# SyncE issues the rotary step's partition-swapping DMAs; the norms' broadcasts and the modulation's columns become TensorE transposes, with sums on VectorE

## The chip, the cores and the metric

The kernel runs on one NeuronCore of a Trainium2 chip. Its time is device microseconds of one launch; the median of three runs stands for a kernel.
## The reference, cut to what matters

One decoder block over a sequence of 1024 tokens with 1024 features, all in float32:

```
mod = silu(c) @ w_ada + b_ada            # 9 sections of 1024, and 2 more for the end
h = rmsnorm(x, g1) * (1 + sc1) + sh1
x = x + 0.5 * gt1 * (silu(h @ w1) * (h @ w3)) @ w2          # feed-forward 1
h = rmsnorm(x, g2) * (1 + sc2) + sh2
q, k, v, B, C, u = split(h @ w_in)
q, k = rope(q), rope(k)                  # t * cos + rotate_half(t) * sin, 64-wide heads
o = (softmax(q1 k1') - lam * softmax(q2 k2')) v             # 4 heads, causal, 128-query blocks
y = B * conv3(C * u)                     # 8 channel groups
x = x + gt2 * concat(rmsnorm(o), rmsnorm(y)) @ w_out
h = rmsnorm(x, g3) * (1 + sc3) + sh3
x = x + 0.5 * gt3 * (silu(h @ w1b) * (h @ w3b)) @ w2b       # feed-forward 2
out = rmsnorm(x, gf) * (1 + scf) + shf
```

## The kernel before, in words

Features lie on the 128 partitions and tokens along the free dimension, in two halves of 512. Large products are split in float32r parts (a rounded high part and the rest), three matmuls of 512 columns for one product; ScalarE makes the high parts and VectorE the low ones. Each engine's order is written out by hand, and semaphores with constant counts tie the engines together. The stages are: a start (about 43 us) with the first norm and the first modulation sections; feed-forward 1 (`up(0)`, then `down(0)`); the convolution groups with their projections; projections of the first head's q and k and of v; four attention heads, `body(hh, ...)`, in whose steps i = 0 to 7 TensorE also projects the next head's q and k; the output projection; feed-forward 2 and the last norm. Matmuls of the feed-forwards stand on line 1536, all others on line 1532, attention's transposes on lines 1956 and 1882.

**The modulation.** During `up`, one section at a time, VectorE multiplies eight loaded tiles of w_ada by the entries of silu(c) and adds them up in `AdaSum` (128 partitions x 1024; 72 tiles, nine sections: six in feed-forward 1, three in 2). What is left is a sum over partitions. `ada_cols` does it on TensorE between two jobs of `up`: eight matmuls of a 128x128 block of `AdaSum` with a column of ones give eight columns in bank 7 of PSUM. Two steps later `ada_bias` on VectorE adds the bias from there (line 1294). A float32 matmul is two MATMUL rows in the profile; a transpose is one.

**The norms.** `mean(q)` sums squares over partitions, ScalarE takes the root, VectorE the reciprocal, and `Spread` holds it repeated over 128 columns. `bcast(q)` (eight uses) and `group_bcast(q)` (eight, in the convolution stage) multiply four 128x128 blocks of `Spread` by the identity `ident`, a part of the tile `Square`, so that every partition gets the row of factors; VectorE then multiplies by it (`nm`, `norm_mul`, and line 1430 for the groups).

**The rotary step.** For head m, part j (two halves each of q and k): ScalarE copies the projection from PSUM into `TmpA` (`raw`, line 871). Then four DMAs swap neighbouring groups of 32 partitions into `TmpG` or `TmpA[:, 1]` (`exchange`, line 877), issued by ScalarE from its own instruction list. GpSimd multiplies with cosines and sines and adds (lines 569, 571, 574). In `body` the four parts fall into the steps i = 1, 2, 4, 5. ScalarE's other work there: exponentials (`exps`, line 899, TensorE's next scores wait for them), copies of transposed blocks (951), of outputs (905), squares (911) and the splitting of a weight unit (`split_hi`, 760). SyncE's list in this stage held only the loads of 29 weight units `Mr` (line 483), each waiting for an older unit to be split.

Of the kernel before, what the change touches and what calls it, by code (L numbers as in the profile page):

```python
# [150 lines left out]
def program(nc, up_w, down_w, units, ada, x_t, cols_d, lam_d, rope_d, square_d, out_t):  # L151
    ctx = ExitStack()
    with ctx:
# [85 lines left out]
        Cols, _ = place("Cols", [P, NCOLS])  # L239
        Mod, _ = place("Mod", [P, SECTIONS * KT])  # L240
        Scale, _ = place("Scale", [P, 4, KT])
        Gate, _ = place("Gate", [P, 3, KT])
# [117 lines left out]
        ada_used, row_used, row_done = sem("ada_used"), sem("row_used"), sem("row_done")  # L360
        cols_done, mod_done, scales = sem("cols_done"), sem("mod_done"), sem("scales")
        lam_done, lam_exp = sem("lam_done"), sem("lam_exp")
# [37 lines left out]
        def _(sp):  # L400
# [79 lines left out]
            sp.dma_start(Rope[:], rope_d).then_inc(rope_loaded, 16)  # L480
            for n in range(RING, UNITS):
                sp.wait_ge(lo_done, n - RING + 1)
                sp.dma_start(Mr[:, n % RING, :], units[n]).then_inc(raw_loaded[n % RING], 16)
            for u in range(2):
                load_up(1, u)
# [114 lines left out]
        def _(act):  # L600
# [272 lines left out]

            def exchange(j, slot, to):

                for a in range(0, P, 32):
                    act.dma_start(to[a:a + 32, :], TmpA[a ^ 32:(a ^ 32) + 32, slot, :]).then_inc(shifted[j % 2], 16)  # L877

            for c in (1, 2):  # L880
                split_hi(U_Q0 + c, job_done, JOBS["v"])
            for j in range(4):
                raw(0, j, 4 + j, JOBS["v"] + j + 1, j % 2, 2)
                act.wait_ge(rraw, j + 1)
                if j >= 2:
                    act.wait_ge(rope_done, j - 1)
                exchange(j, j % 2, TmpG[:, j % 2, :])
                if j % 2:
                    split_hi(U_Q0 + 3 + j // 2, job_done, JOBS["v"] + j + 1)
# [33 lines left out]
            def body(hh, prev, nxt):  # L923

                J, nq, steps = JOBS["att"] + 4 * hh, U_Q1 + 2 * hh, STEP_OF_JOB
                for i in range(QB):
# [26 lines left out]
                    if nxt and i == QB - 1:  # L953
                        exps(0, at + 1)
                    rotated = nxt and i in steps
                    if rotated:
                        act.wait_ge(rraw, hh * 4 + 4 + j + 1)
                        act.wait_ge(rope_done, hh * 4 + 4 + j)
                    if i:
                        square_o(i - 1, at - 1)  # L960
                    if rotated:
                        exchange(j, 0, TmpA[:, 1, :])
                    if rotated and j % 2:
                        split_hi(nq + 2 + j // 2, job_done, J + j + 1)
# [29 lines left out]
        def _(dve):  # L994
# [295 lines left out]

            def ada_bias(s, bank=7):

                dve.wait_ge(cols_done, s + 2 if s else 2)
                nc.vector.tensor_tensor(Mod[:, bass.ts(s, KT)], PS[:, bank, 0:KT], Cols[:, bass.ts(s, KT)], ALU.add)\
                    .then_inc(mod_done, 1)
# [86 lines left out]
            second_bias(0)  # L1382
            ada_bias(SH1, 4)
            second_scale(0)
# [145 lines left out]
        def _(pe):  # L1530
# [7 lines left out]
            def ada_between(ph, t):  # L1538

                for y in range(KT - 1, KT * len(ADA_IN[ph]), KT):  # L1540
                    if ada_step(ph, y) + 2 == t:
                        if y == KT - 1:
                            pe.wait_ge(silu_done, silu_no(ph, 0, 3))
                        ada_cols(ADA_IN[ph][y // KT])
# [79 lines left out]
            def down_free(ph, i, d):  # L1624

                if i >= 2:
                    pe.wait_ge(x_added, 28 * ph + 4 * (i - 2) + d + 1)
                elif i == 0:
                    if d == 0:
                        pe.wait_ge(silu_done, silu_no(ph, NG - 1, 2))  # L1630
                    elif d == 1:
                        pe.wait_ge(dadd, dadd_no(ph, PAIRS - 2, 5))
                    elif d == 2:
                        pe.wait_ge(dadd, dadd_no(ph, PAIRS - 1, 5))
                    else:
                        pe.wait_ge(mul_done, silu_no(ph, NG - 1, 2))
                elif d == 0:
                    pe.wait_ge(mul_done, silu_no(ph, NG - 2, 2))
                elif d == 1:
                    pe.wait_ge(dadd, dadd_no(ph, PAIRS - 3, 5))  # L1640
                elif d == 3:
                    pe.wait_ge(mod_done, 12 if ph else 9)
# [95 lines left out]
            def bcast(q):  # L1738

                pe.wait_ge(spread_done, q + 1)  # L1740
                for b in range(4):
                    made = mm(PS[:, 7 - q % 2, blk(b)], Spread[:, q % NH, blk(b)], ident, True, True)
                made.then_inc(bcast_done, 1)

            def ada_cols(s, bank=7):

                pe.wait_ge(ada_used, (s + 1) * KT)
                for c in range(KT):
                    made = mm(PS[:, bank, c:c + 1], AdaSum[:, blk(c)], Ones[:], True, True)
                made.then_inc(cols_done, 1)  # L1750
# [32 lines left out]
            for cg in range(2):  # L1783
# [287 lines left out]
```

## Time and profile before

| | |
|---|---|
| median of 3 runs | 1884.25 us (1883.03 to 1886.19) |
| the profiled execution's own time | 1886.2 us |
| its span in the trace | 1884.4 us |
| busy: PE, PEld | 1815.4 us (96%), 1470.0 us |
| busy: DVE, ACT, POOL | 1260.8, 773.4, 270.8 us |
| mean granted clock of TensorE | 0.986 |

The span is the time from the first to the last instruction; the rest of an execution's time lies around it. An engine's busy time is not counted while it issues DMAs or waits.

### The profile page before, as it was taken

What the parts mean: (1) busy time and instruction counts of PE and PEld (TensorE: products, weight loads), DVE (VectorE), ACT (ScalarE), POOL (GpSimd) and SP (SyncE); (2) the same over time, 40 slices, a digit from 0 to 9 for tenths busy, and PEclk for the clock granted to TensorE, in tenths of its full rate; (3) what the DMA queues carried; (4) which work ended last, traced back from release to release, by engine and by line L of the source; (5) the groups of instructions that cost most, each with busy time, mean ns of one, the idle gap of its engine ahead of it and who ended that gap; (6) DMA issues with size and microseconds to landing.
All of it is one profiled execution on the core that took longest, in us unless ns stands there. A gap on an engine that the chain in (4) does not pass through costs nothing.

```text
span 1884.4 us, 22925 instructions
## 1 busy us (share of the span) xinstructions
PE 1815.4 (96%) x8248; PEld 1470.0 (78%) x8248; DVE 1260.8 (67%) x1952; ACT 773.4 (41%) x1392; POOL 270.8 (14%) x411
## 2 busy tenths in 40 slices
PE   5999999999999999999999999899999999999997
PEld 2878888888788877888877666787888888888885
DVE  5887777777586776444226668687767766577767
ACT  5643333333344564111125555574333333344445
POOL 2011211211210000000303330201111211111000
PEclk9999999999999999999999999999999999999998
DMA  8165565654864321111201110325454544476432
GB/s 319 69 229 199 206 224 188 242 202 171 272 217 150 96 75 61 44 45 45 77 26 44 45 34 1 134 82 209 157 195 170 207 166 172 167 255 218 128 96 90
DMA packets 100528, 269.76 MB, mean 143 GB/s; under 512 B 13120, under 2 KB 13504, under 8 KB 100288
## 3 DMA queue, kind: packets, MB, share of 16 engines
q1 hardware_dynamic: 62608, 146.30, 22.3%
q0 software_dynamic: 34304, 117.46, 17.9%
q10 hardware_dynamic: 3504, 4.53, 1.0%
q8 instruction: 66, 1.08, 0.2%
q14 instruction: 46, 0.38, 0.1%
HBM read 209.53 MB, written 54.53 MB: 140 GB/s over the span
## 4 chain that ended last, share of the span: by engine, by line
PE 87%; DVE 6%; ACT 3%; issue 1%; DMA 1%; POOL 1%; ACTq 1%; DVEq 0%; POOLq 0%
PE PS L1536 60%; PE PS L1532 26%; DMA AdaFirst<-ada 1%; PE PS L1956 1%; DVE NMax L1447 1%; ACTq L877 1%; DVE Ml L1246 1%; DVE SqSum L1312 0%; DVE TmpA L1330 0%; DVE Wl L1041 0%; DVE Wl L1038 0%; DMA TmpA<-TmpA 0%; DVE CT L1412 0%; ACT PR L899 0%; DVE X L1193 0%
## 5 line engine op out<-in xcount | busy, mean ns | idle before, releaser
L1536 PE MATMUL PS<-Bh,Wh 128*128 128x512 f32 x1120 | 438.0, 391 | 3.8 <-ACT T L659 3.8
L1536 PE MATMUL PS<-Bh,Wl 128*128 128x512 f32 x1120 | 436.6, 390 | 0.0
L1536 PE MATMUL PS<-Bl,Wh 128*128 128x512 f32 x1120 | 436.5, 390 | 0.0
L1536 PEld LDWEIGHTS PS<-Bh,Wh 128*128 128x128 f32 x1120 | 210.5, 188 | 50.1 <-issue 4.1
L1536 PEld LDWEIGHTS PS<-Bh,Wl 128*128 128x128 f32 x1120 | 210.6, 188 | 44.4
L1536 PEld LDWEIGHTS PS<-Bl,Wh 128*128 128x128 f32 x1120 | 210.6, 188 | 43.2
L1536 PE MATMUL PS<-Wh 128*128 128x512 f32 x616 | 240.3, 390 | 3.4 <-DVE Wl L1041 1.7
L1536 PE MATMUL PS<-Wl,Wh 128*128 128x512 f32 x616 | 239.7, 389 | 0.0
L1536 PE MATMUL PS<-Wh,Wl 128*128 128x512 f32 x616 | 239.7, 389 | 0.0
L1038 DVE TENSOR_TENSOR Wl<-RawB,Wh 128x512 fp32r<-128x512 f32 x154 | 106.6, 692 | 135.9 <-ACT Wh L634 134.8
L634 ACT ACTIVATE Wh<-RawB 128x512 fp32r<-128x512 f32 x154 | 97.3, 632 | 229.8 <-PE PS L1536 229.8
L659 ACT ACTIVATE T<-PS 128x512 f32<-128x512 f32 x120 | 71.7, 597 | 248.4 <-PE PS L1536 248.4
L1006 DVE TENSOR_TENSOR Wl<-Sums,Wh 128x512 fp32r<-128x512 f32 x160 | 110.2, 689 | 83.1 <-ACT Wh L624 82.9
L1536 PEld LDWEIGHTS PS<-Wh 128*128 128x128 f32 x616 | 115.6, 188 | 28.4 <-DVE T L1072 2.5
L1536 PEld LDWEIGHTS PS<-Wl,Wh 128*128 128x128 f32 x616 | 115.6, 188 | 24.0
L1536 PEld LDWEIGHTS PS<-Wh,Wl 128*128 128x128 f32 x616 | 115.6, 188 | 24.0
L1532 PE MATMUL PS<-Hh,Mh 128*128 128x512 f32 x320 | 131.9, 412 | 2.2 <-DVE Hl L1336 1.3
L1006 DVE TENSOR_TENSOR Wl<-Raw,Wh 128x512 fp32r<-128x512 f32 x136 | 93.9, 695 | 57.3 <-ACT Wh L624 57.1
L624 ACT ACTIVATE Wh<-Sums 128x512 fp32r<-128x512 f32 x160 | 98.4, 623 | 79.3 <-DVE Sums L1024 65.0
L1532 PE MATMUL PS<-Hl,Mh 128*128 128x512 f32 x320 | 126.9, 397 | 0.0
L1532 PE MATMUL PS<-Hh,Ml 128*128 128x512 f32 x320 | 126.9, 397 | 0.0
L1062 DVE TENSOR_TENSOR T<-T,PS 128x512 f32<-128x512 f32 x120 | 82.1, 684 | 42.0 <-PE PS L1536 38.8
(193 smaller groups left out, 2866.8 us busy)
## 6 DMA issues: line engine op xcount, KB each, us to landing
Raw<-up_w SPq DMA_DIRECT2D x86, 512.0 KB, 5.5
Ada<-ada POOLq DMA_DIRECT2D x72, 512.0 KB, 4.5
g_dram<-T SPq DMA_DIRECT2D x88, 256.0 KB, 2.1
W2s<-down_w POOLq DMA_DIRECT2D x88, 256.0 KB, 4.3
s_dram<-W2s POOLq DMA_DIRECT2D x88, 256.0 KB, 2.5
GQ<-g_dram POOLq DMA_DIRECT2D x88, 256.0 KB, 3.3
RawB<-s_dram SPq DMA_DIRECT2D x88, 256.0 KB, 2.8
RawB<-down_w SPq DMA_DIRECT2D x66, 256.0 KB, 2.7
```

The lines of the kernel that those rows point to most:

```text
L624: nc.scalar.activation(Wh[:, slot, :], src, ACT.Copy).then_inc(w_hi, 1)
L634: nc.scalar.activation(Wh[:, 4 + m % 4, :], RawB[:, m % 8, :], ACT.Copy).then_inc(w_hi, 1)
L659: nc.scalar.activation(T[:, 4 * w + q, :], PS[:, x + (j == 1), :], ACT.Copy).then_inc(acopy, 1)
L877: act.dma_start(to[a:a + 32, :], TmpA[a ^ 32:(a ^ 32) + 32, slot, :]).then_inc(shifted[j % 2], 16)
L1006: nc.vector.tensor_tensor(Wl[:, slot, :], src, Wh[:, slot, :].bitcast(F32), ALU.subtract).then_inc(w_lo, 1)
L1038: nc.vector.tensor_tensor(Wl[:, 4 + m % 4, :], RawB[:, m % 8, :], Wh[:, 4 + m % 4, :].bitcast(F32), ALU.subtract).then_inc(w_lo, 1)
L1062: nc.vector.tensor_tensor(T[:, 4 * w + q, :], T[:, 4 * w + q, :], PS[:, x + (j != 4), :], ALU.add)\
L1246: nc.vector.tensor_tensor(lo, Mr[:, n % RING, :], hi.bitcast(F32), ALU.subtract).then_inc(lo_done, 1)
L1447: nc.vector.tensor_reduce(NMax[:, c:c + 1], scores(c, 0, i + 1), AX.X, ALU.max, negate=True)\
L1532: return nc.tensor.matmul(out, lhs, rhs, start=first, stop=last)
L1536: return nc.tensor.matmul(out, lhs, rhs, start=first, stop=last, skip_group_check=True)
L1956: made = nc.tensor.transpose(PS[:, 4 + r, blk(b % 4)], PR[:, 2, blk(b)], ident)
```

## The change

TensorE's `bcast` and `group_bcast` call `transpose` with the same operands in place of a matmul with the identity. `ada_cols` transposes the eight blocks of `AdaSum` (128x128 each) into banks 6 and 7 of PSUM; VectorE sums them along the free dimension into `ModSum` and then adds the bias, as two instructions with a semaphore between them. The first section (`AdaRow`, bank 4) and `second_cols` stay as they were. The `exchange` DMAs go from ScalarE's list to SyncE's, between the loads of weight units; their waits go with them.

```
@@ SyncE
-            for n in range(RING, UNITS):
+            def load_unit(n):
                 sp.wait_ge(lo_done, n - RING + 1)
                 sp.dma_start(Mr[:, n % RING, :], units[n]).then_inc(raw_loaded[n % RING], 16)
+            def exchange(m, j):
+                slot, to = (0, TmpA[:, 1, :]) if m else (j % 2, TmpG[:, j % 2, :])
+                sp.wait_ge(rraw, 4 * m + j + 1)
+                if m:
+                    sp.wait_ge(rope_done, 4 * m + j)
+                elif j >= 2:
+                    sp.wait_ge(rope_done, j - 1)
+                for a in range(0, P, 32):
+                    sp.dma_start(to[a:a + 32, :], TmpA[a ^ 32:(a ^ 32) + 32, slot, :]).then_inc(shifted[j % 2], 16)
+            for n in range(RING, U_Q0 + 6):
+                load_unit(n)
+            for m in range(HEADS):
+                for j in range(4):
+                    exchange(m, j)
+                    n = (U_Q1 + 3 + 2 * m if m else U_Q0 + 6) + j // 2
+                    if j % 2 and n < UNITS:
+                        load_unit(n)
+                if m == 0:
+                    for n in range(U_Q0 + 8, U_Q1 + 5):
+                        load_unit(n)
@@ ScalarE, head 0 and body
-                act.wait_ge(rraw, j + 1)
-                if j >= 2:
-                    act.wait_ge(rope_done, j - 1)
-                exchange(j, j % 2, TmpG[:, j % 2, :])
...
-                    rotated = nxt and i in steps
-                    if rotated:
-                        act.wait_ge(rraw, hh * 4 + 4 + j + 1)
-                        act.wait_ge(rope_done, hh * 4 + 4 + j)
                     if i:
                         square_o(i - 1, at - 1)
-                    if rotated:
-                        exchange(j, 0, TmpA[:, 1, :])
-                    if rotated and j % 2:
+                    if nxt and i in steps and j % 2:
                         split_hi(nq + 2 + j // 2, job_done, J + j + 1)
@@ VectorE
+            def ada_bias(s):
+                dve.wait_ge(cols_done, s + 2)
+                nc.vector.tensor_reduce(ModSum[:], PS[:, 6:8, :].rearrange("p b (c d) -> p (b c) d", d=P), AX.X, ALU.add)\
+                    .then_inc(mod_sum, 1)
+                dve.wait_ge(mod_sum, s - 1)
+                nc.vector.tensor_tensor(Mod[:, bass.ts(s, KT)], ModSum[:], Cols[:, bass.ts(s, KT)], ALU.add)\
                     .then_inc(mod_done, 1)
@@ TensorE
-                    made = mm(PS[:, 7 - q % 2, blk(b)], Spread[:, q % NH, blk(b)], ident, True, True)
+                    made = nc.tensor.transpose(PS[:, 7 - q % 2, blk(b)], Spread[:, q % NH, blk(b)], ident)
...
-                    made = mm(PS[:, bank, c:c + 1], AdaSum[:, blk(c)], Ones[:], True, True)
+                    made = nc.tensor.transpose(PS[:, 6 + c // 4, blk(c % 4)], AdaSum[:, blk(c)], ident)
...
-                        made = mm(PS[:, 7, blk(b)], Spread[:, q % 2, blk(b)], ident, True, True)
+                        made = nc.tensor.transpose(PS[:, 7, blk(b)], Spread[:, q % 2, blk(b)], ident)
...
-                            pe.wait_ge(silu_done, silu_no(ph, 0, 3))
+                            pe.wait_ge(mul_done, silu_no(ph, 0, 3))
...
-                elif d == 3:
+                elif d == 2:
                     pe.wait_ge(mod_done, 12 if ph else 9)
```

ScalarE's list in head 0, steps i = 2 and 3, before the change (`PR` exponentials, `O` output copy, `DT` transposed block, `Mh` high part of a weight unit; a row is one call, x4 four equal ones):

```order
L871 ACTIVATE TmpA_108<-PS 128x512
L905 ACTIVATE O_89<-PS,RSum_128 128x128
L951 ACTIVATE DT_110<-PS 128x384
L911 ACTIVATE Junk_130,SqO_131<-O_89 128x128
L877 DMA TmpA_108<-TmpA_108 32x512 x4
L760 ACTIVATE Mh_85<-Mr_90 128x1024
L899 ACTIVATE PR_104,Sum_127<-PS,NMax_126 128x640 x2
```

The same place after it:

```order
L896 ACTIVATE TmpA_108<-PS 128x512
L920 ACTIVATE O_89<-PS,RSum_129 128x128
L966 ACTIVATE DT_110<-PS 128x384
L926 ACTIVATE Junk_131,SqO_132<-O_89 128x128
L785 ACTIVATE Mh_85<-Mr_90 128x1024
L914 ACTIVATE PR_104,Sum_128<-PS,NMax_127 128x640 x2
```

The four DMAs, and the two waits ahead of them, no longer stand between the copy of the projection and the unit's split and the next exponentials. They stand in SyncE's list, here from the last load ahead of them to the second head's (before: one row, 29 loads in a row):

```order
L485 DMA Mr<-units 128x1024 x19
L496 DMA TmpG<-TmpA 32x512 x8
L485 DMA Mr<-units 128x1024
L496 DMA TmpG<-TmpA 32x512 x8
L485 DMA Mr<-units 128x1024 x4
L496 DMA TmpA<-TmpA 32x512 x8
L485 DMA Mr<-units 128x1024
```

Each pair of parts (eight DMAs) now lies between two unit loads, and waits for them and they for it. VectorE's list around the bias of the seventh modulation section in `up(1)` (`T` sums of feed-forward products, `Sums` and `Wl` weights in preparation), before:

```order
L1006 TENSOR_TENSOR Wl<-Sums,Wh 128x512
L1062 TENSOR_TENSOR T<-T,PS 128x512
L1294 TENSOR_TENSOR Mod<-PS,Cols 128x8
L1024 TENSOR_TENSOR Sums<-Raw 128x512
L1006 TENSOR_TENSOR Wl<-Sums,Wh 128x512
L1062 TENSOR_TENSOR T<-T,PS 128x512
```

And after:

```order
L1015 TENSOR_TENSOR Wl<-Sums,Wh 128x512
L1071 TENSOR_TENSOR T<-T,PS 128x512
L1308 TENSOR_REDUCE ModSum<-PS 128x8
L1311 TENSOR_TENSOR Mod<-ModSum,Cols 128x8
L1033 TENSOR_TENSOR Sums<-Raw 128x512
L1015 TENSOR_TENSOR Wl<-Sums,Wh 128x512
L1071 TENSOR_TENSOR T<-T,PS 128x512
```

One reduction over 128x1024 is new between two sums that TensorE's next jobs wait for; nothing changed places.

## Rows read from the trace of the kernel before

**Rows 1.** The page's chain that ended last: share of the span by engine.

```profile
PE 87%; DVE 6%; ACT 3%; issue 1%; DMA 1%; POOL 1%; ACTq 1%; DVEq 0%; POOLq 0%
```

**Rows 2.** Windows: length, busy PE, PEld, DVE, ACT, POOL (instructions), clock, DMA share, GB/s.

```profile
100.00:480.00 380.00, 379.81 (x1716) 315.04 (x1715) 279.91 (x403) 134.50 (x236) 75.36 (x140) 1.00 0.59 209
982.00:1037.00 55.00, 52.26 (x276) 38.89 (x273) 35.25 (x67) 28.49 (x76) 17.43 (x13) 0.97 0.14 39
1037.00:1092.00 55.00, 50.32 (x262) 36.82 (x261) 34.79 (x64) 30.09 (x79) 17.35 (x13) 0.97 0.14 39
1092.00:1147.00 55.00, 48.08 (x260) 35.03 (x258) 37.87 (x69) 32.31 (x82) 16.88 (x12) 1.00 0.11 30
1277.00:1650.00 373.00, 372.98 (x1669) 309.11 (x1668) 252.51 (x377) 132.42 (x234) 62.54 (x116) 1.00 0.50 178
```

**Rows 3.** Groups of instructions on PE: count, busy us, mean ns, idle before.

```profile
L1532 PE MATMUL PS<-Ones,AdaSum 128*128 128x1 f32 x160 | 18.6, 245 | 0.0
L1532 PE MATMUL PS<-Square,Spread 128*128 128x128 f32 x128 | 18.1, 287 | 1.0 <-DVE Spread L1321 1.0
```

**Rows 4.** Timeline of PE at a section's columns: start, us, instruction.

```profile
163.19 1.84 PE L1532 MATMUL PS<-Ones,AdaSum 128*128 128x1 f32 x16
164.89 0.49 PE L1536 MATMUL PS<-Bh,Wh 128*128 128x512 f32 x1
```

**Rows 5.** Timeline of PE at eight float32 transposes in attention.

```profile
1034.23 1.06 PE L1882 MATMUL PS<-Square,O 128*128 128x128 f32 x8 [0.16 <-DVE O L1468]
1035.05 0.48 PE L1532 MATMUL PS<-Hh,Mh 128*128 128x512 f32 x1
```

**Rows 6.** Timeline of PE at a group's broadcast.

```profile
741.98 1.05 PE L1532 MATMUL PS<-Square,Spread 128*128 128x128 f32 x8
742.79 0.48 PE L1532 MATMUL PS<-Hh,Mh 128*128 128x512 f32 x1
```

**Rows 7.** Chain in order of time: start and convolution stages.

```profile
17.91 18.84 PE PS L1532 x56
...
735.48 7.57 PE PS L1532 x40
...
750.42 27.30 PE PS L1532 x128
```

**Rows 8.** Timeline, the last norm's broadcast.

```profile
1872.86 2.08 PE L1532 MATMUL PS<-Square,Spread 128*128 128x128 f32 x8 [1.03 <-DVE Spread L1321]
```

**Rows 9.** Timeline of ACT in head 0, steps i = 2 and 3.

```profile
994.79 0.51 ACTq L877 DMA_DIRECT2D TmpA<-TmpA  x1
995.33 2.25 ACTq L877 DMA_DIRECT2D TmpA<-TmpA  x3
997.69 1.06 ACT L760 ACTIVATE Mh<-Mr 128x1024 fp32r<-128x1024 f32 x1 [2.54 <-issue]
```

**Rows 10.** Timeline of PE, the scores behind it in three heads.

```profile
999.57 0.69 PE L1532 MATMUL PS<-QK 64*128 64x512 f32 x1 [0.90 <-ACT PR L899]
...
1053.04 1.47 PE L1532 MATMUL PS<-NextK,NextQ 64*128 64x512 f32 x3 [1.11 <-ACT PR L899]
...
1107.66 0.69 PE L1532 MATMUL PS<-QK 64*128 64x512 f32 x1 [0.85 <-ACT PR L899]
```

**Rows 11.** Groups of instructions on DVE: widest reduction from PSUM, and bias.

```profile
L1447 DVE TENSOR_REDUCE NMax<-PS 128x1 f32<-128x1024 f32 x8 | 9.8, 1224 | 0.3
L1294 DVE TENSOR_TENSOR Mod<-PS,Cols 128x8 f32<-128x8 f32 x10 | 1.6, 160 | 4.5 <-PE PS L1532 4.5
```

**Rows 12.** Timeline of DVE and PE at two biases in `up`.

```profile
480.08 0.69 DVE L1038 TENSOR_TENSOR Wl<-RawB,Wh 128x512 fp32r<-128x512 f32 x1 [8.82 <-ACT Wh L634]
...
1395.77 0.16 DVE L1294 TENSOR_TENSOR Mod<-PS,Cols 128x8 f32<-128x8 f32 x1
...
1397.89 0.69 DVE L1062 TENSOR_TENSOR T<-T,PS 128x512 f32<-128x512 f32 x1
...
1400.41 0.39 PE L1536 MATMUL PS<-Bh,Wh 128*128 128x512 f32 x1
```

More of the change, by code:

```diff
@@ L240, in program @@
         Mod, _ = place("Mod", [P, SECTIONS * KT])
+        ModSum, _ = place("ModSum", [P, KT])
         Scale, _ = place("Scale", [P, 4, KT])
@@ L360, in program @@
         ada_used, row_used, row_done = sem("ada_used"), sem("row_used"), sem("row_done")
-        cols_done, mod_done, scales = sem("cols_done"), sem("mod_done"), sem("scales")
+        cols_done, mod_sum, mod_done, scales = sem("cols_done"), sem("mod_sum"), sem("mod_done"), sem("scales")
         lam_done, lam_exp = sem("lam_done"), sem("lam_exp")
@@ L872, in raw @@
                                      scale=DH ** -0.5 if j < 2 else 1.0).then_inc(rraw, 1)
-            def exchange(j, slot, to):
-                for a in range(0, P, 32):
-                    act.dma_start(to[a:a + 32, :], TmpA[a ^ 32:(a ^ 32) + 32, slot, :]).then_inc(shifted[j % 2], 16)
             for c in (1, 2):
@@ L1289, in second_scale, with first_bias @@
                                                col("g1", KH * n, KH), ALU.add, ALU.mult).then_inc(scales, 1)
-            def ada_bias(s, bank=7):
-                dve.wait_ge(cols_done, s + 2 if s else 2)
-                nc.vector.tensor_tensor(Mod[:, bass.ts(s, KT)], PS[:, bank, 0:KT], Cols[:, bass.ts(s, KT)], ALU.add)\
+            def first_bias():
+                dve.wait_ge(cols_done, 2)
+                nc.vector.tensor_tensor(Mod[:, 0:KT], PS[:, 4, 0:KT], Cols[:, 0:KT], ALU.add).then_inc(mod_done, 1)
+            def ada_bias(s):
[4 more added lines that the diff above has]
+                nc.vector.tensor_tensor(Mod[:, bass.ts(s, KT)], ModSum[:], Cols[:, bass.ts(s, KT)], ALU.add)\
                     .then_inc(mod_done, 1)
@@ L1382, in _ @@
             second_bias(0)
-            ada_bias(SH1, 4)
+            first_bias()
             second_scale(0)
@@ L1741, in bcast, with ada_cols @@
                 for b in range(4):
-                    made = mm(PS[:, 7 - q % 2, blk(b)], Spread[:, q % NH, blk(b)], ident, True, True)
+                    made = nc.tensor.transpose(PS[:, 7 - q % 2, blk(b)], Spread[:, q % NH, blk(b)], ident)
                 made.then_inc(bcast_done, 1)
-            def ada_cols(s, bank=7):
+            def ada_cols(s):
                 pe.wait_ge(ada_used, (s + 1) * KT)
                 for c in range(KT):
-                    made = mm(PS[:, bank, c:c + 1], AdaSum[:, blk(c)], Ones[:], True, True)
+                    made = nc.tensor.transpose(PS[:, 6 + c // 4, blk(c % 4)], AdaSum[:, blk(c)], ident)
                 made.then_inc(cols_done, 1)
```

## The prediction

> **What bounds the kernel now.** I read the page's chain first: 87% of the span is TensorE, 6% VectorE, 3% ScalarE [rows 1]. So an instruction that leaves TensorE's list is worth its whole length wherever TensorE does not wait anyway, and an instruction that leaves another engine is worth nothing unless TensorE stood waiting for it. Then I asked for the stretches. In the two `up` stages TensorE is busy 379.81 of 380 us and 372.98 of 373 us, VectorE about 280 and 253 us [rows 2]. There all nine modulation sections are summed. In the three attention stretches that also carry projections, TensorE is idle 2.7, 4.7 and 6.9 us of 55 [rows 2]: what ScalarE, VectorE and GpSimd do can show there, and only there up to that much. Last I went to the places that the edit touches.
>
> **Columns of the modulation: matmuls become transposes.** From the first column matmul of a section to the feed-forward matmul behind it, 1.70 us pass (163.19 to 164.89) for 16 MATMUL rows [rows 4]. They have one column each, so it is their 128x128 weight loads that take the time. Afterwards there are 8 rows, of 128 columns. This kernel has the same thing in attention: eight float32 transposes take 0.82 us from their start to that of the next matmul (1034.23 to 1035.05) [rows 5]. So a section saves 1.70 - 0.82 = 0.88 us. Nine sections: 7.9 us, all in stretches in which TensorE has no idle time to absorb it. Of the 160 rows of this kind [rows 3], 144 go; the other 16 belong to the second section's `second_cols` and stay.
>
> **What it adds on VectorE.** A reduction over 128x1024 from PSUM takes 1.22 us where the kernel has one already, and the bias stays at 0.16 us [rows 11]; with the wait between the two I count 1.3 us more a section, 11.7 us in all. I cost it at nothing, because something covers it: VectorE has 100 us free in the first `up` and 120 us in the second [rows 2]. The cover must hold locally too. TensorE's tight wait is for the sum `T` of two jobs before. The bias nearest ahead of such a sum is that of the seventh section: bias at 1395.77, sum 1397.89 to 1398.58, and the job that waits for it starts at 1400.41 [rows 12], 1.83 us later. With 1.3 us more ahead of it, less what VectorE idled, the sum is still in time. The other tight place is at the end of `up(0)`, where the kernel's last bias comes before VectorE's 8.82 us of idling [rows 12]. If the cover were gone, each section would cost up to 1.3 us on TensorE; zero is the one end, 11.7 us the other, and I take zero.
>
> **Broadcasts: half the rows.** A broadcast has 8 MATMUL rows, 0.81 us from its start to the next matmul (741.98 to 742.79) [rows 6]; 128 rows are 16 broadcasts [rows 3]. Afterwards there are 4. By the transposes (0.82 us for eight, 0.10 to 0.11 us each) [rows 5], 0.38 to 0.4 us stay, so 0.42 us is saved at full clock. Which of the 16 lie on the path? The two at the start stand inside an unbroken TensorE piece, 17.91 + 18.84 us [rows 7]; I take 0.6 us for both and not 0.84, since what follows starts at the low clock and may cover more of it. In the convolution stage the chain runs through TensorE up to each group's multiplication by the broadcast (pieces of 7.57 and 27.30 us are two of them) [rows 7], so all eight count; so do that of the second half's norm ahead of this stage and the two around the output projection: 11 x 0.42 = 4.6 us. The last one runs at 1.2 GHz with nothing behind it but the end: 2.08 us for eight rows [rows 8], of which a fixed 0.24 us is the pipeline's (1.05 against 0.81 in [rows 6]); half the rest is 0.9 us. The two in the last part of each `down` lie beside a long chain of ScalarE and VectorE work: between 0 and 0.84 us, I take 0.4. Sum: 0.6 + 4.6 + 0.9 + 0.4 = 6.5 us.
>
> **Partition swaps leave ScalarE.** In head 0, step i = 2, ScalarE issues from 994.79 to 997.58, then splits a weight unit from 997.69, and only then makes the exponentials [rows 9]; TensorE's scores at 999.57 wait 0.90 us for them, and in the next two heads 1.11 and 0.85 us at the same place [rows 10]. Without the DMAs (2.8 us) the exponentials are early, and those gaps close: 2.9 us. Lower bound nothing, if VectorE's maxima, which ScalarE also needs, come as late; upper bound the gaps themselves, as TensorE is the bound on both sides of them. The other idle time of the stretches [rows 2] belongs to VectorE's chain at step i = 6 and to the head change, where no swap stands ahead: unchanged. The issue time itself, some 2.5 us for each of 16 swaps, is worth no more than this, for ScalarE is busy only about half of those stretches [rows 2]. On SyncE the swaps wait between unit loads. Queued behind a late load would be the swap, GpSimd's rotation and the next head's first scores; behind a late swap a load. Every load there waits for the split of a unit that is done before the next part's projection, and the swap may now start at the copy's end, not behind ScalarE's other work. I take zero for it.
>
> **The sum** against the profiled execution's own 1886.2 us: 7.9 + 6.5 + 2.9 = 17.3 us, so 1868.9 us. That execution was 1.95 us above the median of the runs shown; I apply the sum to the median: 1884.25 - 17.3 = 1867 us, 0.9% faster.
>
> **Rivals.**
> *The swaps give nothing* (another wait, the maxima or GpSimd, fills the same gaps): 1867 + 2.9 = 1870 us. For it: VectorE is as busy as ScalarE there [rows 2]. Against it: the 2.54 us before the split is issuing alone [rows 9].
> *VectorE becomes late* in `up`, and TensorE waits in every section: 1.3 us x 9 = 11.7 us lost, 1879 us. For it: tight waits exist at all; against it: 1.83 us of room and 26% free [rows 2, 12].
> *The clock, which ends on the other side.* TensorE's granted clock is 1.0 through both `up` stages and 0.97 in two attention stretches [rows 2]: 3% of 55 us is 1.65 us lost in a stretch with one fall. Attention's stretches hold the kernel's only transposes, idle gaps too. If a run of transposes let the clock fall each time as there, at 25 places instead of none, it would cost 25 x 1.65 = 41 us: 1867 + 41 = 1908 us. It decides from 13 such falls on ((17.3 + 3.8) / 1.65). Against it: three stretches with 36 and more transposes each have two falls among them, and the third, with as many transposes and the most idle time, has clock 1.00 [rows 2].
> The Trainium skill ("TensorE: Matmul & The Clock Gate", Part 4, PE-mode transpose) says that transposes do not count as TensorE work for its clock, which would speak for this rival. By that rule alone the time is the rival's; by the rows, in which full-rate transposes stand in a stretch at 1.00, it is the sum's.
> *The transposes don't save* (a float32 transpose as long as the two rows it replaces): only the swaps remain, 1884.25 - 2.9 = 1881 us. Against it stands the direct row, 0.82 us for eight [rows 5].
>
> **How the numbers follow.** The sum as it stands 0.68; swaps give nothing 0.15; VectorE late in part or whole 0.08; clock falls at many places 0.06, half of these slower than before; transposes don't save 0.03. The measurement of this kernel tells a change from none at about 0.2%, 3.8 us. Faster by more than that: the first three and a part of the rest, 0.93; within it 0.03; slower 0.04. Falls of the clock come and go with the gaps around them: one or two, 1.65 us each, either way, which with the two open terms of 0.4 us spans 1863 to 1871 for the likeliest case alone. With the swaps giving nothing and a fall too (1873.5), and VectorE's term in part, the range is 1862 to 1875 us.
>
> **What would show it.** In the profile after: eight MATMUL rows with `AdaSum` a section, about 0.8 us to the next feed-forward matmul, no new TensorE idle behind them and a clock of 1.00 in `up`; a reduction of about 1.22 us with `ModSum` on VectorE; four rows with `Spread` a broadcast in 0.4 us; no DMA rows on ScalarE in attention, and no wait of the scores for exponentials at step i = 3 in three heads. I am wrong if new idle time appears before feed-forward jobs with VectorE's `T` as its releaser, if the granted clock falls in `up`, or if GpSimd's rotation waits longer for SyncE's swaps than for ScalarE's and the next head's first scores wait for it.

## The result, and the profile after

| | before | after |
|---|---|---|
| median, runs side by side | 1884.03 us (1883.03 to 1886.19, 4 runs) | 1860.4 us (1858.88 to 1863.07, 4 runs) |
| ratio, 95% interval | | 0.9872, 0.9857 to 0.9887 |
| the profiled execution | 1886.19 us | 1858.88 us |
| its span, mean granted clock | 1884.4 us, 0.986 | 1857.1 us, 0.991 |
| busy: PE, DVE, ACT, POOL | 1815.4, 1260.8, 773.4, 270.8 us | 1788.9, 1271.0, 774.3, 268.2 us |

The change gains 23.6 us, 1.3%. The forecast was 1867.0 us, with a range from 1862 to 1875 us: the direction holds, and the time lies below the range. The two profiled executions stand 27.3 us apart, more than the medians; how far single executions of one kernel differ is shown under experiments 12 to 16.

The windows of the profile after (columns as in [rows 2]: length, busy us of PE, PEld, DVE, ACT, POOL, then the granted clock), for the first `up`, three attention stretches and the second `up`:

```profile
100.00:480.00 380.00, 379.76 (x1697) 314.03 (x1697) 292.01 (x419) 135.96 (x239) 75.95 (x141) 1.00 0.60 210
969.00:1020.00 51.00, 48.08 (x265) 35.28 (x262) 32.89 (x64) 28.04 (x75) 16.16 (x12) 1.00 0.15 42
1020.00:1071.00 51.00, 47.76 (x262) 34.97 (x261) 35.60 (x65) 30.25 (x77) 16.52 (x12) 1.00 0.15 42
1071.00:1122.00 51.00, 48.29 (x263) 35.44 (x262) 34.69 (x67) 30.40 (x77) 16.17 (x12) 1.00 0.12 32
1255.00:1627.00 372.00, 371.98 (x1652) 307.50 (x1651) 257.06 (x381) 132.88 (x234) 62.78 (x117) 1.00 0.50 178
```

TensorE is still busy all through both `up` stages, at clock 1.00: VectorE's new reductions bring it no wait, and no fall of the clock stands at the nine runs of transposes. Groups of instructions after, answering to [rows 3, 11] (count, busy us, mean ns, idle before):

```profile
L1766 PE MATMUL PS<-Square,AdaSum 128*128 128x128 f32 x72 | 9.3, 272 | 0.0
L1308 DVE TENSOR_REDUCE ModSum<-PS 128x8 f32<-128x1024 f32 x9 | 11.0, 1219 | 1.8 <-PE PS L1766 1.8
L1311 DVE TENSOR_TENSOR Mod<-ModSum,Cols 128x8 f32<-128x8 f32 x9 | 1.5, 168 | 0.3
L1819 PE MATMUL PS<-Square,Spread 128*128 128x128 f32 x32 | 4.8, 272 | 0.0
L1759 PE MATMUL PS<-Square,Spread 128*128 128x128 f32 x32 | 5.5, 298 | 1.5 <-DVE Spread L1338 1.5
```

PE's timeline after (start, length, instruction) at the places of [rows 4, 6, 8], a section, a group's broadcast and the last norm:

```profile
161.73 1.03 PE L1766 MATMUL PS<-Square,AdaSum 128*128 128x128 f32 x8
162.52 0.48 PE L1553 MATMUL PS<-Bh,Wh 128*128 128x512 f32 x1
...
734.23 0.60 PE L1819 MATMUL PS<-Square,Spread 128*128 128x128 f32 x4
734.58 0.48 PE L1549 MATMUL PS<-Hh,Mh 128*128 128x512 f32 x1
...
1846.53 1.11 PE L1759 MATMUL PS<-Square,Spread 128*128 128x128 f32 x4 [1.03 <-DVE Spread L1338]
```

From its first transpose to the matmul behind it a section takes 0.79 us (162.52 - 161.73) in place of 1.70, a broadcast 0.35 in place of 0.81, the last one 1.11 in place of 2.08.

ScalarE's timeline after, in head 0 at the steps of [rows 9]:

```profile
980.46 0.19 ACT L926 ACTIVATION_READ_ACCUMULATOR Junk<-O 128x1 f32 x1
980.55 1.05 ACT L785 ACTIVATE Mh<-Mr 128x1024 fp32r<-128x1024 f32 x1
982.34 0.80 ACT L914 ACTIVATE PR<-PS,NMax 128x640 f32<-128x640 f32 x1 [0.74 <-DVE NMax L1464]
```

The split follows at once, and ScalarE now waits 0.74 us for VectorE's maxima, so these come next in line, as one rival had it, but early enough. PE's scores behind it in three heads, answering to [rows 10]:

```profile
985.80 1.57 PE L1549 MATMUL PS<-QK 64*128 64x512 f32 x8
987.30 0.50 PE L1549 MATMUL PS<-Hh,Mh 128*128 128x512 f32 x1
...
1036.97 1.57 PE L1549 MATMUL PS<-NextK,NextQ 64*128 64x512 f32 x8
...
1088.04 1.57 PE L1549 MATMUL PS<-QK 64*128 64x512 f32 x8
```

No wait is left. And the rows say more than that: all eight score matmuls are through in 1.57 us.

**Where the time went.** The clock of TensorE blurs such a comparison, as the experiments show. I therefore compare with a second profile of the kernel before (e_before_2 below, span 1880.3 us), whose granted clock was 0.5 for 17.1 us in all between 60 and 1830 us, near the 13.7 us of the profile after. Each stretch runs between the same two matmuls in both (start to start); both have clock 1.00 all through it:

| stretch | before | after | saved | forecast |
|---|---|---|---|---|
| six sections in the first `up` | 105.31 to 479.16 | 103.70 to 471.96 | 5.6 us | 5.3 |
| three sections in the second | 1253.60 to 1806.18 | 1233.75 to 1783.66 | 2.7 us | 2.6 |
| six of the eight groups' broadcasts | 775.71 to 902.94 | 765.50 to 890.16 | 2.6 us | 2.5 |
| from head 0's step i = 2 to head 2's end | 996.79 to 1131.24 | 985.60 to 1113.02 | 7.0 us | 2.9 |

The spans differ by 23.2 us. Of the 5.3 us outside these stretches 1.4 us are net effects of falls of the clock that only one of the two has (+1.5, -1.6 and +1.5 us at three places); what is left, 3.9 us, I put down to the other ten broadcasts (forecast 4.0); it is a remainder, in which differences at the start and at the clock's falls are mixed. So columns gave 8.3 us (forecast 7.9), broadcasts 6.5 (6.5), of which 2.6 are read directly, and the partition swaps 7.0 (2.9).

### The profile page after: what moved, and what is told of

Read it like the earlier page. It is cut to its first block, busy times and chain, and to the rows that moved or that the text cites. A ratio compares the mean times of both kernels' runs of the same rounds, so it can differ in the third digit from the quotient of the medians.

```text
span 1857.1 us, 22662 instructions
## 1 busy us (share of the span) xinstructions
PE 1788.9 (96%) x8112; PEld 1445.0 (78%) x8112; DVE 1271.0 (68%) x1961; ACT 774.3 (42%) x1392; POOL 268.2 (14%) x411
## 3 DMA queue, kind: packets, MB, share of 16 engines
q8 instruction: 65, 1.06, 0.2%
## 4 chain that ended last, share of the span: by engine, by line
PE 86%; DVE 8%; ACT 3%; issue 1%; DMA 1%; POOL 0%; ACTq 0%; DVEq 0%; POOLq 0%
PE PS L1553 60%; PE PS L1549 24%; DVE NMax L1464 1%; PE PS L1973 1%; DMA AdaFirst<-ada 1%; DVE X L1360 1%; DVE SqSum L1329 1%; DVE Ml L1255 1%; DVE TmpA L1347 1%; DVE Wl L1050 0%; PE PS L1766 0%; DVE Wl L1047 0%; DVE Wl L1015 0%; DVE X L1202 0%; DVE PR L1478 0%
## 5 line engine op out<-in xcount | busy, mean ns | idle before, releaser
L571 POOL DMA_DIRECT2D s_dram<-W2s x88 | 48.2, 547 | 412.8 <-DVE W2s L1093 412.8
```

The costliest lines, as they stand in the source:

```text
L571: pool.dma_start(s_dram[ph][x // 4, n], W2s[:, n, :]).then_inc(w2_stored[n], 16)
```

## Experiments

Each kernel was timed in turn with the kernel before on the same chip. "The parts" are the change's own pieces.

**1 to 3. One part at a time on the kernel before.** e_cols has only the changes of `ada_cols` and `ada_bias` and their semaphores, e_bcast only `transpose` in `bcast` and `group_bcast`, e_swap only the diff's SyncE and ScalarE parts.

> The kernel before with the modulation's columns alone changed (transposes into banks 6 and 7, reduction and bias on VectorE). Theory A, the gain is the shorter TensorE insertion and nothing else: 0.91 us in each of nine sections, 8.2 us, so about 1876 us; granted clock 1.00 in both up stages, no new idle time behind the sections. Theory B, part of the surplus over my sum comes from the clock (fewer falls once the transposes are in): more than 8.2 us, by steps of 1.65 us. Theory C, VectorE's extra 11.7 us costs something: less than 8 us.

> The kernel before with the 16 broadcasts alone changed. Theory A: 0.45 us for each broadcast on the path: two at the start, eight groups, three norms, and about 0.9 us for the last, 6.5 to 7 us, about 1877.5 us. Theory B, the broadcasts change where the clock falls (convolution stage, end): up to 1.65 us more or less for each fall gained or lost.

> The kernel before with the partition swaps alone moved to SyncE. Theory A (my prediction's): the three gaps of TensorE at step i = 3 close, 2.9 us, about 1881 us. Theory B: the second map's scores were late there too; with both exponentials in time the two maps' score matmuls start together (as in the changed kernel, 985.80 and 985.81 us), 0.76 us a head more, so 5.4 us, about 1878.6 us. Either way a fall of the clock in attention may go as well, 1.65 us each.

| | median | ratio, 95% interval | saved |
|---|---|---|---|
| e_cols | 1876.37 us (7 runs) | 0.9949, 0.9930 to 0.9968 | 7.9 us |
| e_bcast | 1876.48 us (5 runs) | 0.9959, 0.9946 to 0.9971 | 7.8 us |
| e_swap | 1876.08 us (5 runs) | 0.9958, 0.9946 to 0.9970 | 8.2 us |

The medians add up to 23.9 us, near the change's gain of 23.6; each has an uncertainty of some 2 to 4 us (the seven runs of e_cols alone spread from 1868.69 to 1879.78 us). Columns agree with their forecast; the broadcasts' 6.5 us lies inside their interval (5.5 to 10.2 us); the swaps' 2.9 us lies outside theirs (5.7 to 10.2 us). So the miss is mainly in the swaps, and they show it without the other parts. The traces say the same, stretch by stretch of the table above, against e_before_2: in e_cols the two stretches with the nine sections are 8.3 us shorter, in e_bcast the six groups 2.6 us and in e_swap the three heads 7.9 us (126.53 us in place of 134.45), while in all three kernels the sections and groups that the part doesn't touch take the same time within 0.1 us. Only the three heads of e_cols and e_bcast, each with one fall of the clock in them, take 1.0 and 0.8 us less without a reason that I looked for.

**Why the swaps give more: the trace.** PE's timeline at the scores of the three heads in e_before_2, to be held against the changed kernel's above:

```profile
998.08 2.33 PE L1532 MATMUL PS<-QK 64*128 64x512 f32 x8 [1.01 <-ACT PR L899]
1000.34 0.50 PE L1532 MATMUL PS<-Hh,Mh 128*128 128x512 f32 x1
...
1051.48 2.33 PE L1532 MATMUL PS<-NextK,NextQ 64*128 64x512 f32 x8 [1.20 <-ACT PR L899]
...
1104.74 2.33 PE L1532 MATMUL PS<-QK 64*128 64x512 f32 x8 [0.98 <-ACT PR L899]
```

The same eight matmuls take 2.26 us to the next one before (998.08 to 1000.34), and 1.50 us after (985.80 to 987.30). They are the scores of two softmax maps, four each, with 64 rows of the array apiece, and each map's matmuls wait for that map's exponentials. After, both maps' matmuls start together (985.80 and 985.81), before, the second 0.53 us behind the first (998.08 and 998.61), since it waits for the second exponentials. Views of PE that end 0.2 to 0.3 us behind the block's start show it, e_before_2 and then the changed kernel, where two matmuls have begun:

```profile
998.08 0.69 PE L1532 MATMUL PS<-QK 64*128 64x512 f32 x1 [1.01 <-ACT PR L899]
```

```profile
985.80 0.71 PE L1549 MATMUL PS<-QK 64*128 64x512 f32 x2
```

So late exponentials cost a gap and then a block in which the maps run less side by side: the block ends 1.85, 2.03 and 1.82 us later in the three heads, 5.7 us, of which 0.76 us each, 2.3 us, lie inside the block. The gap itself is not the same in every execution: in head 0 it is 0.90, 1.61, 1.01 and 1.50 us in the four profiles of the kernel before, and the three together are 2.9 to 3.7 us; the block is 2.26 us in the heads of all four.

The remaining 1.3 us of the 7.0 stand at step i = 6. VectorE's timeline there, e_before_2, head 0:

```profile
1019.03 1.95 DVE L1246 TENSOR_TENSOR Ml<-Mr,Mh 128x1024 fp32r<-128x1024 f32 x1
1020.90 0.15 DVE L1454 RECIPROCAL RSum<-Sum 128x2 f32<-128x2 f32 x1
1021.09 0.22 DVE L1456 SCALAR_TENSOR_TENSOR Ratio<-RSum,LamS,Sum 128x1 f32<-128x1 f32 x1
1021.34 1.28 DVE L1461 SCALAR_TENSOR_TENSOR PR<-PR,Ratio 128x1024 f32<-128x1024 f32 x1
```

and GpSimd and PE of the same profile:

```profile
1018.63 1.27 POOL L574 TENSOR_TENSOR NextK<-NextK,TmpA 128x512 f32<-128x512 f32 x1
...
1022.68 1.09 PE L1956 MATMUL PS<-Square,PR 128*128 128x128 f32 x8 [1.26 <-DVE PR L1461]
```

The same places in e_swap:

```profile
1017.19 1.26 POOL L597 TENSOR_TENSOR NextK<-NextK,TmpA 128x512 f32<-128x512 f32 x1
...
1018.50 1.22 DVE L1253 TENSOR_TENSOR Ml<-Mr,Mh 128x1024 fp32r<-128x1024 f32 x1
...
1021.42 1.09 PE L1963 MATMUL PS<-Square,PR 128*128 128x128 f32 x8 [0.53 <-DVE PR L1468]
```

VectorE's split of a weight unit takes 1.22 us when GpSimd has ended before it begins, and 1.95 us when GpSimd's last rotation instruction still runs for 0.87 us (to 1019.90); TensorE waits behind it, 0.53 against 1.26 us. Swaps issued early end the rotation early. The Trainium skill ("SBUF — State Buffer", Who interferes with whom) says that a VectorE instruction with two SBUF inputs contends with a GpSimd instruction that reads SBUF, and calls the ports that they share an exclusive lock. These rows agree: 0.87 us of overlap cost VectorE 0.73 us, and 0.67 us of it in the changed kernel's head 0 cost 0.53 us, while GpSimd's instruction took 1.26 or 1.27 us in each case. In the changed kernel the splits take 1.75, 1.66 and 1.22 us in the three heads and TensorE waits 1.06, 0.98 and 0.53 us, in each case 0.68 or 0.69 us less than the split is long. In e_swap all three take 1.22 us, which is why the swaps gave 7.9 us there and 7.0 us here.

**4. Does VectorE have the room?**

```
+                for n in range(3):
                     nc.vector.tensor_reduce(ModSum[:], ...).then_inc(mod_sum, 1)
...
```

> The changed kernel with VectorE's reduction of each modulation section done three times in a row instead of once, 2.5 us more in each of nine sections. If VectorE's room covers it: no change against the changed kernel, about 1860 us. If the room is only just enough for one reduction: up to 2.5 us x 9 = 22 us more, and TensorE idle before feed-forward jobs with VectorE's sums as releaser.

Measured: 1863.41 us (4 runs), ratio 0.9889 (0.9876 to 0.9902), with 33.0 us of reductions in place of 11.0, and 1.4 to 3.0 us above the changed kernel's two medians. Against the changed kernel's trace TensorE lost time at two of the nine sections, 1.20 and 1.13 us. So I was wrong that three cost nothing, but they cost only a tenth of their 22 us more; that one costs nothing is seen in the stretches above, where each section saved its full 0.9 us.

**5 and 6. Which swap matters?** e_swap_j1 puts only part j = 1 of heads 1 to 3 on SyncE, e_swap_rest all the others and not those three.

```
+        def on_sync(m, j):
+            return m > 0 and j == 1          # e_swap_rest: m == 0 or j != 1
```

> The kernel before with only the part j = 1 of heads 1 to 3 (step i = 2, three of the 16 swaps) issued by SyncE, the other 13 by ScalarE as before. If what the change gains in attention is the lateness of the exponentials of step i = 3 in these three places (gap, second map's scores, and the clock's falls behind them): nearly the whole of what all 16 gave, 5 to 8 us, about 1877 to 1879 us, and no fall of the clock between the attention heads. If ScalarE's issue time is worth something everywhere: about 3/16 of it, 1.5 us.

> The complement: the other 13 swaps issued by SyncE, those three by ScalarE. If the three places are all: about the time of the kernel before, 1884 us, within 1.5 us, TensorE's gaps before the scores of step i = 4 as before. If issue time counts everywhere: 6 us less. A third possibility: the first part's swap, now earlier on SyncE, lets GpSimd end earlier, so that ScalarE waits less for it at step i = 2; then the gaps shrink and some of the gain comes here too.

Measured: 1878.41 us (8 runs), ratio 0.9962 (0.9950 to 0.9975), and 1876.56 us (6 runs), 0.9955 (0.9937 to 0.9973). In both traces the gap before the scores is closed in all three heads. That one part would carry it was wrong as an "only"; the third possibility is what came. Nor did the closed gaps keep the clock up: e_swap_j1's profile has two falls between the attention heads. ScalarE in e_swap_rest shows why the other swaps help as well:

```profile
992.73 0.49 ACT L980 ACTIVATE DT<-PS 128x384 f32<-128x384 f32 x1
992.99 0.60 ACTq L905 DMA_DIRECT2D TmpA<-TmpA  x1
...
995.62 1.06 ACT L788 ACTIVATE Mh<-Mr 128x1024 fp32r<-128x1024 f32 x1 [2.10 <-issue]
996.58 0.78 ACT L928 ACTIVATE PR<-PS,NMax 128x640 f32<-128x640 f32 x1
```

The issuing is still there, but it begins at once. In e_before_2 ScalarE first stood idle for 1.57 us until GpSimd had done with the part ahead:

```profile
993.13 0.31 ACT L911 ACTIVATE Junk<-O 128x128 f32<-128x128 f32 x1 [1.57 <-POOL NextQ L574]
```

In e_swap_rest, with that part's swap on SyncE GpSimd is through by 991.33. The delay had two pieces, a wait of 1.57 us and 2.5 to 2.9 us of issuing, and taking away either closes the gap. The split at i = 6 keeps its 1.95 to 1.98 us in e_swap_j1 and takes 1.22 us in e_swap_rest: that share belongs to the later parts.

**7 and 8. Is it ScalarE's time?** The changed kernel, with n small copies on ScalarE where part j = 1 was issued.

```
+                    if nxt and i in steps and j == 1:
+                        for n in range(8):            # e_work12: 12 here and in the wait
+                            nc.scalar.activation(Extra[:], Rope[:, 0, 0:P], ACT.Copy).then_inc(extra, 1)
+                            act.wait_ge(extra, 8 * hh + n + 1)
```

> The changed kernel with eight small copies (128x128, each waited for, about 2.6 us in all, the length of the four issues) on ScalarE where the swap of part j = 1 stood; they write a tile that nothing reads. If ScalarE's time alone held up the exponentials: the gaps of the kernel before come back, 5.4 us more than the changed kernel and a fall or two of the clock, 1866 to 1868 us. If the wait for GpSimd ahead of the issue was a needed part of it (the changed kernel's exponentials are some 2.2 us early): the first scores are in time and only the second map's late, 0 to 2.3 us more, 1860 to 1863 us.

> The changed kernel with twelve small copies (about 4.0 us, by eight that took 2.69) on ScalarE in each of the three heads where it used to issue a swap and to wait for GpSimd. Removed wait and issues were together 1.57 + 2.8 = 4.4 us; eight copies (2.7 us) brought no gap back. If the gaps come of ScalarE's time before its exponentials and nothing else, there was room of about 3.4 us before PE waits (4.4 less the gap of 0.97): twelve copies bring back 0.4 to 0.8 us a head before the scores and some of the 0.76 us by which the score block was shorter, 1.5 to 4 us in all, so 1862 to 1867 us, and the exponentials of head 0 begin about 1.3 us later than with eight. Rival (the gaps come of the queue or of the DMAs' landing): no gap at all, 1860 to 1864, as with eight.

Measured: 1863.61 us (5 runs), ratio 0.9884 (0.9868 to 0.9900), with no wait before the scores; and 1867.33 us (6 runs), 0.9903 (0.9884 to 0.9921). PE's scores of head 0 with eight copies and with twelve:

```profile
988.81 1.70 PE L1555 MATMUL PS<-QK 64*128 64x512 f32 x8
```

```profile
989.07 2.33 PE L1555 MATMUL PS<-QK 64*128 64x512 f32 x8 [0.66 <-ACT PR L916]
```

Copies of 2.69 us bring no gap and delay the second map by 0.14 us; copies of 4.06 us bring back 0.66 us of gap and the long block, with no DMA on that queue. Relative to the changed kernel this is 0.75 + 0.77 us in head 0's trace. The 5.3 us over the changed kernel timed beside it (e_after_again) are above the upper end of what I expected; 4.5 us of them are the three blocks with their gaps. So ScalarE's time before its exponentials is enough to make the gap and the long block; neither the queue nor the DMAs' landing is needed for it.

**9 and 10. The changed kernel again, and without the swaps.**

> The changed kernel once more, nothing edited. Theory 1 (the mechanism gives about 18 us by the steps between the matmuls of the two traces, and what is over that is stretches at the granted clock of 0.5 that this kernel's executions happen to have fewer of): the median comes within 1860 to 1865 us again, and in the new profiled execution the PE rows before the scores of heads 0 to 2 at query block 4 are without a wait again (score block 1.50 us, not 2.26), while its stretches at 0.5 clock may stand in other places and sum to anything between 14 and 31 us. Theory 2 (the change itself does away with the stretches at 0.5): the new profile again shows only three such stretches, about 14 us, in the same places.

> The changed kernel with ScalarE issuing the partition swaps of the rotary step again; the transposed columns and broadcasts stay. If the parts add up (columns and broadcasts gave 7.9 and 7.8 us by medians when each was alone): 1884.0 - 15.7 = 1868.3 us, so 1866 to 1870.5, and 5 to 8 us above the changed kernel. In the trace the three gaps of 0.9 to 1.1 us before the scores of heads 0 to 2 are back, and the block of eight score matmuls takes 2.26 us again, 5.4 us in all. Rival (the swaps' gain of 8 us seen alone was mostly a matter of the clock): 1863 to 1866, with those gaps back all the same. Rival (the other two parts need the swaps on SyncE, and lose part of their gain without): above 1871.

Measured: e_after_again 1862.04 us (6 runs), ratio 0.9881 (0.9859 to 0.9903); e_no_swap 1873.02 us (6 runs), 0.9929 (0.9907 to 0.9951), 11.0 us more. From the transposes ahead of head 0's scores (982.17, and 979.35 in the changed kernel) to VectorE's `PR` at step i = 6 of head 2 (1120.41 and 1109.81), e_no_swap takes 7.8 us more than the changed kernel, with gaps of 1.96, 1.01 and 0.96 us and the 2.26 us blocks back; head 0's gap is the longest of all profiles. I had forecast 5.4 us, from shorter gaps and without the split of step i = 6, and 1868.3 us; 1873 lies in my rival's zone (parts that need each other), but its interval (1866 to 1874 us) holds both. By these stretches the parts add up; by the times alone it isn't settled.

**11. One block later for VectorE's split.** An attempt at a faster version.

```
-                    if nxt and i - 1 in steps and steps.index(i - 1) % 2:
-                        split_lo(nq + 2 + steps.index(i - 1) // 2)
+                    if nxt and i in (3, QB - 1):
+                        split_lo(nq + 2 + i // (QB - 1))
```

> The changed kernel with VectorE's second split of a head's keys moved one query block later, from before to after the scores whose probabilities wait for VectorE. In the changed kernel's trace PE idles 1.06, 0.98 and 0.53 us in heads 0 to 2 for VectorE's PR, which stands behind that split. Theory: these three close, up to 2.6 us, so 1858 us (1856.5 to 1860.5), if the split is still in time for the next head's scores. Rival (PE waits as long for the next thing, VectorE's DT before it at the head's last step, or the split itself is late for the next head): same as the changed kernel or up to 2 us slower, 1860 to 1863, with the wait moved to the last query block or to the head's change.

Measured: 1863.42 us (6 runs), ratio 0.9878 (0.9855 to 0.9901): as the changed kernel. In the first trace no head has a gap for `PR`, but that is not the edit's doing: its clock fell to 0.5 just ahead of that place in all three heads, and the unedited kernel with the same three falls (e_after_2) has no such gap either. Only head 2 of e_late_split_2 has clock 1.00 there. PE in it, and in the unedited kernel's e_after_again:

```profile
1112.54 1.09 PE L1973 MATMUL PS<-Square,PR 128*128 128x128 f32 x8
1114.99 0.50 PE L1549 MATMUL PS<-Gh,Mh 128*128 128x512 f32 x1 [1.35 <-DVE Ml L1255]
```

```profile
1110.85 1.09 PE L1973 MATMUL PS<-Square,PR 128*128 128x128 f32 x8 [0.53 <-DVE PR L1478]
```

There the edit took away the gap of 0.53 us, and the next matmul waited 1.35 us for the late split, in both traces. So the rival was right for head 2: the wait moved, and grew. What the edit does at clock 1.00 in heads 0 and 1 no trace shows.

**12 to 16. The clock.** The first profiles suggested that the change also rid the kernel of falls of the clock. I looked at more executions of unedited kernels, and once more at e_late_split.

> The kernel before once more, unchanged, for a second profile. If the falls of TensorE's clock in the attention heads follow from the gaps, there are one or two falls between 980 and 1110 us again, though perhaps in other places; if they are chance, there may be none.

> The kernel before, unedited, one more profiled execution, for the stretches at the granted clock of 0.5 between 60 and 1830 us: its two profiles so far have 30.7 and 37.5 us of them. Theory 1 (what the change gained beyond the steps between the matmuls is that its executions have fewer such stretches): 27 us or more again. Theory 2 (chance of which execution was profiled): anything from 14 to 37 us, as with the changed kernel.

> The kernel before, unedited, a further profiled execution: as for the other one, 27 us or more at the granted clock of 0.5 between 60 and 1830 us if the change did away with some of them, anything from 14 to 37 us if the two first profiles differed from the changed kernel's by chance. The span less half of it is 1867 to 1869 us in either case.

> The changed kernel, unedited, one more profiled execution, for its stretches at the granted clock of 0.5 between 60 and 1830 us: its two profiles so far have 13.7 and 20.5 us. Theory 1 (it has fewer of them than before): under 24 us again. Theory 2 (chance): anything from 14 to 37 us. Under both, the span less half of those stretches is 1847 to 1851 us, and the stretches fall in other places than in the first two.

> The changed kernel with VectorE's second split of a head's keys one query block later, one more profiled execution. Its first had 34.1 us at the granted clock of 0.5 between 60 and 1830 us and a span of 1864.6 us; its fastest timed executions took 1858.9 us. If those stretches come by chance: 14 to 24 us of them here, and a span of 1855 to 1860 us. If the edit itself brings them: 30 us or more again, above 1862 us.

| profile | span | at clock 0.5 between 60 and 1830 us |
|---|---|---|
| before: page, look, 2, 3 | 1884.4, 1886.1, 1880.3, 1881.4 us | 30.7, 37.5, 17.1, 17.1 us |
| changed: page, again, 2 | 1857.1, 1857.8, 1863.9 us | 13.7, 20.5, 37.5 us |
| late split: first, 2 | 1864.6, 1860.3 us | 34.1, 20.5 us |

Theory 1, fewer falls, is refuted as I had put it (27 us or more before, under 24 after): the means are 25.6 and 23.9 us, and either kernel has executions at both ends. With four and three profiles a difference of a few us can't be ruled out. That the falls between the heads follow from the gaps fails too: e_before_2 and e_before_3 have the gaps and no fall between 980 and 1110 us. The second profile of the late split has 20.5 us, as chance would have it and not the edit, with a span 0.3 us above what I expected. My method failed too: the span less half of those stretches should have been constant, and went from 1867.3 to 1872.9 us for the kernel before and from 1845.2 to 1850.3 for the changed one. By the spans, 17 us more at 0.5 cost the kernel before 4.4 us (means 1880.9 and 1885.2) and 20 us more cost the changed one 6.4 (1857.5 and 1863.9): about 0.3 us for each, not 0.5. One reason can be seen: some of these stretches lie just ahead of a wait of TensorE's and use it up. In e_after_again the clock was 0.5 from 1005.4 and from 1056.6 us, and the waits of 1.06 and 0.98 us for `PR` at step i = 6 of heads 0 and 1 are gone there, while head 2, at clock 1.00, keeps its 0.53 us. At like clock, the two kernels are 21 to 23 us apart.

## Why the prediction missed

- **Columns: right.** 0.88 us a section and 7.9 us in all were forecast; 0.91 us and 8.3 us measured in the traces, 7.9 us by the medians of e_cols.
- **VectorE's reductions cost nothing: right**; the room holds most of three times as much, but not all (experiment 4). Their 1.22 us was right too.
- **Broadcasts: right.** 6.5 us forecast and measured, though 3.9 us of the measured are a remainder, so that the exact agreement is luck; alone they gave 7.8 us (5.5 to 10.2). In `down` 0.5 us was gained before its last part and 0.4 given back there by a gap that grew (1.74 to 2.15 us in the first), within the 0 to 0.84 us foreseen.
- **Partition swaps: the step that failed**, as a mis-sized term: 2.9 us forecast, 7.0 us measured by trace, 8.2 us (5.7 to 10.2) alone. The mechanism was right: the exponentials come early and the three gaps close. Wrong was "upper bound the gaps themselves, as TensorE is the bound on both sides of them", a bound that the prediction gave no row for. TensorE was busy behind the gap, but for longer: the second map's scores waited for the second exponentials, and the two maps lost 0.76 us of side-by-side work each time, 2.3 us. The trace of the kernel before had this length: the block at 999.57 is one row of 2.33 us, x8, with the next matmul at 1001.83. The prediction's rows [rows 10] don't show it, since their views end inside the blocks; their x1 and x3 are only as many matmuls as had begun by then. And that the other idle time stays "unchanged" was wrong by 1.3 us: GpSimd's earlier end shortened VectorE's split at i = 6. The last 0.5 us is the size of the gaps: the first matmuls of the three blocks were 3.4 us late in all in e_before_2, against the changed kernel, and not 2.9; the gaps vary from one execution to the next. The prediction also left out ScalarE's wait of 1.57 us for GpSimd ahead of the issuing, but the gaps close without it.
- **The swaps on SyncE at no cost: right.** GpSimd's waits for swaps from the second head on sum to 35.2 us in place of 51.2, and neither trace lists a wait for a unit's load; the gap at the heads' change is 0.41 us in both traces.
- **The clock rival: refuted.** The clock is 1.00 in both `up` stages with nine runs of eight transposes. The allowance of one or two falls either way was too small for single executions, whose spans differ by 6 to 7 us for one kernel, but in the medians it was not what failed.
- **Sum.** 17.3 us forecast; with the swaps at 7.0 it is 21.4, or 1862.9 us from the same median, and with the columns at 8.3 too 21.8, or 1862.4 us. The measured medians, 1860.4 and 1862.04 us, lie 2.0 and 0.4 us below that. The side-by-side ratios leave room for it: they say a gain of 21.3 to 26.9 us and, in e_after_again, 18.3 to 26.6 us. So the swaps' term explains 4.1 of the 6.6 us by which the median missed 1867; about 2 us are not assigned to anything and lie within the noise. The range ended at 1862, since the swaps' gain was capped at the gaps.

## What to carry to other kernels

A gap in front of a busy engine is not an upper bound for what its cause is worth: compare the block behind the gap with the same block where nothing is late, since instructions that could run side by side may be released one by one. Ask for a view that reaches past the block: a row counts only what began inside the view. When an engine's instruction is moved, ask which instruction of the engines behind it then overlaps with which. For effects of a few microseconds take several profiles of each kernel, and compare stretches between the same instructions where the clock agrees; a wait that is gone may have been used up by a slower clock ahead of it.

## What the runs showed of the hardware

- At the granted clock of 1.00, a float32 transpose of 128x128 costs TensorE 0.10 us in a run of eight (0.79 us) and is one row; the matmul with the identity took two rows and 0.20 us (0.81 us for four blocks).
- The granted clock stayed at 1.00 over the transposes in `up`. The Trainium skill's sentence that they do not count as work for the clock ("TensorE: Matmul & The Clock Gate", Part 4) would have let one expect a fall at them; none is to be seen in either `up`, where each run of transposes is 0.8 us between full matmuls. Longer runs were not tried.
- Score matmuls with 64 rows each ran side by side when both were ready: eight in 1.50 us, and 2.26 us when one map came 0.53 us late.
- VectorE's 128x1024 instruction with two SBUF inputs took 1.22 us, 1.75 us with a GpSimd instruction over its first 0.67 us, and 1.95 us with one over its first 0.87 us.
- Executions of the kernel before with 17 us more at a granted clock of 0.5 took 4.4 us longer, and one of the changed kernel with 20 us more took 6.4 us longer.
- Issuing four DMAs took ScalarE 2.8 us (994.79 to 997.58), and the same four SyncE 2.41 us; the profile's busy time of ScalarE doesn't hold it.
